# Half of the front projection's chunks by three rounded products, with the key and value rows parked in DRAM, and a reordered end of a down projection

## The reference, cut to what matters

```
h = rmsnorm(x, norm_g)
q, kvc, kvs, kvw, gt, z, xbc, dtr = split_cols(h @ w_in, EVEN_SPLITS)
...
o_nsa = nsa_mixer(q, sigmoid(gt), past_cmp + kvc, past_slc + kvs, win + kvw, ...)
o_ssm, ssm_new, conv_new = mamba_mixer(z, xbc, dtr, conv0, ssm0, ...)
x = x + jnp.concatenate([o_nsa, o_ssm], axis=-1) @ w_out
...
x + (jax.nn.silu(g) * u) @ w_down
```

## Time and profile before

| what | value |
|---|---|
| median of three runs | 2692.76 us |
| profiled execution | 2691.72 us, span 2689.5 us |
| PE busy | 2628.4 us, 98% of the span |
| DVE / ACT / POOL busy | 59% / 42% / 38% |
| x, q, z pieces (L633) | 242.4 us busy, 150.6 to 475.2 us |
| longest wait of PE | 6.6 us, L2358 for DVE L3203, at 1610 us |

### The profile page before, as it was taken

One profiled execution on the slowest core, in us unless ns is written; L12 is line 12 of the kernel. 1 busy time (PEld: TensorE's weight loads), 2 busy tenths in 40 slices (PEclk: granted clock), 3 DMA queues, 4 the chain that ended last, 5 costly groups with the idle time before them and its releaser, 6 DMA issues.

```text
span 2689.5 us, 51117 instructions
## 1 busy us (share of the span) xinstructions
PE 2628.4 (98%) x20404; PEld 2372.7 (88%) x20404; DVE 1589.9 (59%) x2577; ACT 1131.1 (42%) x2373; POOL 1019.5 (38%) x844
## 2 busy tenths in 40 slices
PE   8999999999989999999999999999999999999998
PEld 6866667666669999999999999978999999999998
DVE  3222256777554576667677772186277666676775
ACT  4022213666552644444434342076164444443335
POOL 2431000222223388777730021236148777771000
PEclk9999999999999999999999999999999999999999
DMA  7754310310434222223276331100313222238533
GB/s 234 206 168 155 93 32 1 116 33 2 121 104 155 73 94 93 98 87 116 94 246 205 92 90 41 35 21 17 97 53 113 94 97 98 85 102 295 165 92 105
DMA packets 256591, 283.78 MB, mean 106 GB/s; under 512 B 43098, under 2 KB 192656, under 8 KB 255507
## 3 DMA queue, kind: packets, MB, share of 16 engines
q1 hardware_dynamic: 245840, 247.84, 29.3%
q0 software_dynamic: 7616, 30.14, 3.7%
q10 hardware_dynamic: 2898, 2.54, 0.3%
HBM read 214.25 MB, written 71.32 MB: 106 GB/s over the span
## 4 chain that ended last, share of the span: by engine, by line
PE 65%; DVE 4%; issue 1%; POOL 1%; ACT 1%; DMA 1%; SPq 0%; DVEq 0%; POOLq 0%; ACTq 0%
PE ps L2541 31%; PE ps L3114 16%; PE ps L2342 8%; PE ps L2358 3%; PE ps L3454 1%; PE ps L3314 1%; DVE part L2701 1%; PE ps L3435 1%; PE ps L3418 1%; PE ps L2045 1%; PE ps L2010 1%; PE ps L1998 1%; DVE d_blo L3058 0%; DMA arena<-in_w_gate_up 0%; DVE spot L3229 0%
## 5 line engine op out<-in xcount | busy, mean ns | idle before, releaser
L2541 PE MATMUL ps<-part,block_hi 128*128 128x272 f32 x4768 | 792.1, 288 | 6.8 <-POOL block_lo L2829 5.6
L2541 PEld LDWEIGHTS ps<-part,block_hi 128*128 128x128 f32 x4768 | 675.6, 189 | 8.0 <-issue 7.3
L2541 PE MATMUL ps<-part,block_lo 128*128 128x272 f32 x2672 | 531.0, 289 | 0.0
L2829 POOL TENSOR_TENSOR block_lo<-arena,block_hi 128x512 fp32r<-128x512 f32 x296 | 444.6, 1532 | 51.2 <-ACT block_hi L2596 44.6
L2541 PEld LDWEIGHTS ps<-part,block_lo 128*128 128x128 f32 x2672 | 409.1, 189 | 1.0 <-issue 1.0
L3114 PE MATMUL ps<-d_bhi,d_whi 128*128 128x272 f32 x1232 | 255.1, 288 | 1.3 <-POOL d_wlo L3063 0.8
L3114 PE MATMUL ps<-d_blo,d_whi 128*128 128x272 f32 x1232 | 255.2, 288 | 0.0
L3114 PE MATMUL ps<-d_bhi,d_wlo 128*128 128x272 f32 x1232 | 254.5, 288 | 0.0
L633 PE MATMUL ps<-arena 128*128 128x352 f32 (+1 forms) x768 | 242.4, 473 | 0.0
L2596 ACT CAST block_hi<-arena 128x512 fp32r<-128x512 f32 x296 | 167.1, 619 | 151.7 <-POOL arena L2844 90.8
L633 PEld LDWEIGHTS ps<-arena 128*128 128x128 f32 x768 | 144.4, 191 | 85.0 <-issue 3.8
(11 more groups left out here) (516 smaller groups left out, 4671.1 us busy)
## 6 DMA issues: line engine op xcount, KB each, us to landing
arena<-in_w_gate_up SPq DMA_DIRECT2D x176, 256.0 KB, 3.8
spare_sb<-a_keep SPq DMA_DIRECT2D x78, 272.0 KB, 2.8
arena<-a_keep SPq DMA_DIRECT2D x64, 272.0 KB
arena<-in_w_down SPq DMA_DIRECT2D x16, 1024.0 KB, 7.1
a_keep<-arena SPq DMA_DIRECT2D x58, 272.0 KB, 2.1
arena<-in_cache_nsa_slc_kv SPq DMA_DIRECT2D x112, 128.0 KB, 2.5
a_keep<-spare_sb SPq DMA_DIRECT2D x52, 272.0 KB, 2.0
arena<-in_cache_nsa_cmp_kv SPq DMA_DIRECT2D x109, 128.0 KB, 2.3
```

Source lines behind the costliest of these rows:

```text
L2541: mm = nc.tensor.matmul(ps[:, b + j, 0:QT], y, z[:, j * QT:(j + 1) * QT], start=first and m == 0, stop=last and m == 2)
L2829: p.tensor_tensor(block_of(q, "lo", a), block_f[q % 2]["lo", a], block_of(q, "hi", a).bitcast(F32), ALU.subtract).then_inc(sem("up_lo"), 1)
```

## The change

In every x, q and z piece, the first four chunks (`FK`) are no longer one plain float32 matmul but three rounded ones: weights hi x input hi, weights hi x input lo, weights lo x input hi. The other four chunks stay as they were. The parts come from new instructions:

- ACT rounds the four input chunks to `f_hi` (128x1088 each), and DVE subtracts to get `f_lo` (128x1088 each), once.
- For each of the 8 panels 3 to 10, ACT rounds half of it (`high_part`, 128x1024) and DVE subtracts (`low_part`, 128x1024). The calls stand at fixed places in the two engines' programs. PE waits for the DVE part before the panel's first piece.
- Room: there are two panel slots and not three, so that panel n waits until panel n - 2 is done. `f_hi` lies over `kvt`, so that the key and value rows are parked: ACT writes them to a DRAM tensor `kv_keep` before `f_hi` is made, POOL's stores to the outputs read from there, SP loads the keys for the transposes after the last but one panel is done (`turn_key`, 1 MB), and all rows back to `kvt` after the transposes, ahead of `bias_in`.
- At the end of layer 0's down projection, the four `low` calls no longer stand ahead of the evictions, but one behind each.

```
-SLOTS = 3
+SLOTS = 2
...
+        def high_part(act, n):
+            act.wait_ge(w_ready[n % SLOTS], w_count[n])
+            nc.scalar.copy(fw_hi[n % 2], wp[n % SLOTS][:, 0:FK].rearrange("p c n -> p (c n)")).then_inc(sem("f_hi"), 1)
+        def low_part(dve, n):
+            dve.wait_ge(*reached("f_hi", FK + n - FP0 + 1))
+            raw = wp[n % SLOTS][:, 0:FK].rearrange("p c n -> p (c n)")
+            nc.vector.tensor_tensor(fw_lo[n % SLOTS], raw, fw_hi[n % 2].bitcast(F32), ALU.subtract).then_inc(sem("f_split"), 1)
...
+                        for m, (w, x) in enumerate(((fw_hi[n % 2], f_hi), (fw_hi[n % 2], f_lo), (fw_lo[n % SLOTS], f_hi))):
+                            mm = nc.tensor.matmul(out[:, 0:b - a], w[:, c], x[k][:, a:b], start=k == 0 and m == 0, stop=False)
...
                     self.w = self.E.next_panel()
+                    if kind != "kv":
+                        pe.wait_ge(*reached("f_split", FK + self.E.panel - FP0))
...
+            act.dma_start(kv_kept[:, 0:PT], kvt[:, 0:PT]).then_inc(sem("kv_moved"), 16)
+            act.wait_ge(*reached("kv_moved", 32))
+            step_wait(act, "dve", "h_normed")
+            for k in range(FK):
+                nc.scalar.copy(f_hi[k], hT[:, k]).then_inc(sem("f_hi"), 1)
...
             weights(PROJ0)
+            sp.wait_ge(*panel_done[PROJ0 - 2])
+            sp.dma_start(turn_key, kv_kept[:, 0:PT].rearrange("p i (b n) -> p i b n", b=2)[:, :, :, 0:P])...
             sp.wait_ge(sem("keys_tr"), 1)
+            sp.dma_start(kvt[:, 0:PT], kv_kept[:, 0:PT]).then_inc(sem("kv_moved"), 16)
+            sp.dma_start(kvt[0:TS, PT], kv_kept[0:TS, PT]).then_inc(sem("kv_moved"), 16)
             load(sp, "bias_in")
...
                 if c:
                     state_and_output(c - 1)
+                if c in (1, 4):
+                    low_part(dve, FP0 + 6 + c // 4)
...
                 evict(SSM_PIECES[c])
+                if c in (0, 3):
+                    high_part(act, FP0 + 6 + c // 3)
...
-            for u in range(0 if l else QUADS):
-                low(u)
...
                 evict(len(D_ORDER) - 1, 0)
+                low(0)
                 for k in range(1, QUADS):
                     evict(len(D_ORDER) - 1, k)
                     add_square(3 * QUADS + k - 1)
+                    low(k)
```

More of the change, by code:

```diff
@@ L70 @@
 KH = KC // 2
+FK = KC // 2
+FP0 = 3
 HT = T // 2
@@ L231, in build @@
         o_hi_end = rounded(b0, ["o_hi6", "o_hi7"], [T] * 2)
+        f_hi, f_lo = rounded(kv2, [f"f_hi{k}" for k in range(FK)], [T] * FK), spots[0:FK]
+        fw_hi = rounded(w0 + SLOTS * KC * WCOL, ["fw_hi0", "fw_hi1"], [FK * WCOL] * 2)
+        fw_lo = [rounded(w0 + s * KC * WCOL, [f"fw_lo{s}"], [FK * WCOL])[0] for s in range(SLOTS)]
         PART, BLOCK = KH * HT, KH * P
@@ L415, in dense_slot, with totals @@
             return (n + (n >= DOWN[0])) % WSLOTS
-        def totals(pieces, slots, slot_of):
+        def totals(pieces, slots, slot_of, first=None):
             total, out = [0] * slots, []
             for n, p in enumerate(pieces):
-                total[slot_of(n)] += 16 * len(p(wp[0] if n or slots == WSLOTS else w_kv0))
+                total[slot_of(n)] += 16 * len(p(first if first is not None and n == 0 else wp[0]))
                 out.append(total[slot_of(n)])
             return out
-        w_count, wd_count = totals(panels, SLOTS, lambda n: n % SLOTS), totals(dense, WSLOTS, dense_slot)
+        w_count, wd_count = totals(panels, SLOTS, lambda n: n % SLOTS, w_kv0), totals(dense, WSLOTS, dense_slot)
         wd_ready = [sem(f"wd_ready{k}") for k in range(WSLOTS)]
@@ L632, in one @@
                         a, b = SPLIT[i]
-                        mm = nc.tensor.matmul(out[:, 0:b - a], self.w[:, k, u % 2 * P:(u % 2 + 1) * P], hT[:, k, a:b],
-                                              start=k == 0, stop=k == KC - 1)
+                        if k >= FK:
+                            mm = nc.tensor.matmul(out[:, 0:b - a], self.w[:, k, u % 2 * P:(u % 2 + 1) * P], hT[:, k, a:b],
+                                                  start=False, stop=k == KC - 1)
+                            continue
+                        n = self.E.panel - 1
+                        c = slice(k * WCOL + u % 2 * P, k * WCOL + (u % 2 + 1) * P)
+                        for m, (w, x) in enumerate(((fw_hi[n % 2], f_hi), (fw_hi[n % 2], f_lo), (fw_lo[n % SLOTS], f_hi))):
+                            mm = nc.tensor.matmul(out[:, 0:b - a], w[:, c], x[k][:, a:b], start=k == 0 and m == 0, stop=False)
                 if k1 == KC:
@@ L876, in front_dve @@
             i.then_inc(sem("front_dve"), 1)
+            for k in range(FK):
+                dve.wait_ge(*reached("f_hi", k + 1))
+                v.tensor_tensor(f_lo[k], hT[:, k], f_hi[k].bitcast(F32), ALU.subtract).then_inc(sem("f_split"), 1)
+            for n in (FP0, FP0 + 1):
+                low_part(dve, n)
             dve.wait_ge(sem("w1_used"), W1_CHUNKS)
@@ L891, in front_dve @@
                     values_dve(dve, E, 0)
+                if c in (2, 4, 6):
+                    low_part(dve, FP0 + 1 + c // 2)
             keys_dve(dve, E, 1)
@@ L1163, in front_sp @@
             cache_pages(sp, 0, 22, 42)
-            weights(SLOTS)
+            weights(FP0)
             sp.wait_ge(sem("x_spilled"), 16)
@@ L1167, in front_sp @@
             cache_pages(sp, 0, 64, 72)
[L1168 removed]
+            weights(FP0 + 2)
             sp.wait_ge(sem("w1_used"), W1_CHUNKS)
             cache_pages(sp, 1, 80, 104)
[L1171 removed]
+            weights(FP0 + 3)
             cache_pages(sp, 1, 104, 128)
[L1173 removed]
+            weights(FP0 + 5)
             sp.wait_ge(sem("w1_used"), 2 * W1_CHUNKS)
@@ L1291, in turn_keys @@
             n = tile_n(i)
-            return nc.tensor.transpose(key_bank(br, i), kvt[0:n, i, 256 * br:256 * br + P], ident[0:n, 0:n])
+            keys = turn_key[:, i, br] if i < PT else turn_tail[0:n, br]
+            return nc.tensor.transpose(key_bank(br, i), keys, ident[0:n, 0:n])
         def first_keys_pe(pe, piece):
@@ L1379, in ssm_dve @@
             operands(PT)
+            low_part(dve, FP0 + 5)
             dve.wait_ge(sem("s0t_used"), NB)
```

42 lines of the change are left out of this document (29 added, 13 removed), and 2 rows, old and new, of the table SERVED.

## The result

| | before | after |
|---|---|---|
| median of 22 runs each | 2688.95 us | 2696.19 us |
| lowest to highest | 2685.48 to 2699.89 | 2691.54 to 2707.52 |
| ratio, 95% interval | | 1.0024, 1.0014 to 1.0034 |
| the profiled execution, its span | 2691.72, 2689.5 | 2692.47, 2690.8 |

The account below looks back on a forecast made before the run. PE was taken as the bound, but by only 2 to 3 us. A 22.8 us saving on the pieces, less waits, copies and clock loss, summed to +3.3 us on 2691.72 us, giving 2695.0 us, range 2679 to 2708 us.

Parts of the forecast that it names:

- pieces: x, q and z pieces on PE: three rounded products per chunk replace a plain one in 16 units, -22.8 us.
- the compression's weights: Before the first piece: these weights travel at the same time as the parking, +0.5 us (0 to 2).
- second batch's rows: Before the second batch's hidden steps: PE comes earlier and waits for rows POOL lays, copies meeting DVE's taps, +5.5 us.
- ACT's copies: In the scan: ACT's rounding copies delay the first state copy and a shorter filler piece uncovers ACT's chain, +0.85 us.
- turn 1: Scan turn 1: PE's pieces wait for ACT's copy and DVE's subtraction behind its outputs, +4.9 us.
- turn 4: Scan turn 4: PE's pieces wait for ACT's copy and DVE's subtraction behind its outputs, +5.2 us.
- the attention's start: First attention score: bias tables queue behind 2.1 MB of restored rows, +5.5 us (4.5 to 7.5).
- the down projection's end: PE's wait for the last eviction there: new order of subtractions and evictions gives -0.4 us (-3 to +3).
- the clock: PE's granted clock falls behind four new waits, +4 us (bounds 0 and 11).
- Rival 3: Rounded pieces: weight loads set the pace, 12.7 us more for 576 matmuls, sum +16 us, 2708 us; chance 0.05.
- rival 2: Attention's start: restored rows take 16 us, first score 16 us late, sum +14 us, 2706 us; chance 0.06.
- Rival 1: At the new waits: they are covered and most of the gain stays, 2675 us; chance 0.10.

Follow-up runs that it names:

- panel_later: The changed kernel with panel 4 loaded after the first batch's last product, its parts made in the first round of pieces; 1.0010 of the kernel before.
- before_down: The kernel before, with only its down projection's end changed: four banks read first, one subtraction between second and third; 0.9970 of the kernel before.
- three: The changed kernel with bias tables ahead of restored rows, panel 9 and 10 parts a turn earlier, one piece before the second batch's hidden steps; 0.9933, 2672.8 us.
- down_last: The changed kernel with the down projection's four banks read first, one subtraction between second and third, the rest behind; 0.9990 of the kernel before.
- five: The changed kernel with tables first, parts earlier, one piece moved ahead, panel 4 later and the down projection's banks read first; 0.9903 of the kernel before, 2662.7 us.
- bias_first: The changed kernel with the two bias tables loaded ahead of the restored key and value rows; 1.0008 of the kernel before.
- low_early: The changed kernel with the parts of panels 9 and 10 made a turn ahead of their use; 0.9976 of the kernel before.

## Why the prediction was right, point by point

2695.0 us was forecast and 2696.19 us measured; the working gave +3.3 us and the runs +6.5 us. That the two times lie 1.2 us apart is in part luck: the forecast was added to one execution of 2691.72 us, 2.8 us above the median of the 22 runs before, and its sum was 3.2 us too small. The terms, in us, by the stages above:

| term | forecast | measured |
|---|---|---|
| pieces | -22.8 | -21.9 (16 units of 1.37, read between the hidden steps) |
| the compression's weights | +0.5 | +2.3 (mean of ten traces; 1.2 in the profiled one) |
| second batch's rows | +5.5 | +3.75 |
| ACT's copies | +0.85 | +0.9 (0.46 before the key products, 0.4 in the turns) |
| turn 1 | +4.9 | +4.6 (0.95 and 3.69) |
| turn 4 | +5.2 | +4.7 |
| the attention's start | +5.5 | +6.9 |
| the down projection's end | -0.4 | -0.7 |
| the clock | +4 | +5.7 (1.05 rows, 2.25 turns, 2.36 attention) |
| sum | +3.3 | +6.3 |

- **The pace of the pieces** was right to 4%: rounded matmuls at 0.16 to 0.17 us as in the earlier trace rows. Rival 3, that the weight loads would set the pace, is refuted. The pass rule of the Trainium skill (FP8 and Floating Point Precision, TensorE Precision Notes) gave an estimate of 1.85 us a unit; the trace gives 1.37 us, so the measured pace of another stage was the better source.
- **The weights of the compression** are the term that was mis-sized: +2.3 us, outside the 0 to 2 us that I gave. I had taken the parking as the only load there. With two slots, panel 4 starts at 122.45 us, as the parking does at 123.02 us, and I did not put the two together. panel_later shows that the loss goes when panel 4 is moved. The making of the parts cost nothing, as forecast: PE does not wait before its first piece.
- **The rows**: both halves were right in kind. POOL's copies did meet DVE's taps (6.58 us for 4.68), as the page SBUF — State Buffer of the Trainium skill has it (SBUF: two separate sides). But POOL began them 55.7 us behind the first piece (57.0 us before), and PE's first piece itself stood 2.7 us later than in the kernel before (153.31 against 150.57 us), while the copies began only 1.5 us later; so the wait was 3.75 us and not 5.5. One step here was wrong: I had called SP's wait for the sixth piece free, by 1.4 us, and SP waited 1.8 us, with the second batch's pages behind it. Without that, PE's wait would be up to 1.8 us shorter, an estimate; no run tests it.
- **Turns 1 and 4** came as worked out, to 0.5 us, in place, cause and size.
- **The attention's start** lay within its bounds (4.5 to 7.5). The restored 2048 KB landed in 8.0 us; rival 2, which needed 15.5 us, is refuted.
- **The down projection's end** came as worked out, and I took it for done. What before_down shows is that the same place held 8 us that the change did not touch (L1649 to the first products: 1132.30 us before, 1124.32 us there).
- **Rival 1**, covered waits, is refuted by the four waits themselves. Its 2675 us is what `three` reaches once they are covered.
- **Slips that move no term**: the measured pace is above that of the pass rule by 12 ns a matmul (0.106 us over the 9 matmuls of a chunk), not 15. The windows of the earlier trace rows put the fall of the clock at about 1612.3 us and its return at 1622.5 us, 5.7 us after PE began again.
- What is not settled: which of ACT's small waits belong to the copies, and 0.2 us of the sum. The start-up differs between executions by more than any term but the pieces (the row transposes begin between 120.67 and 131.41 us), so single executions prove nothing about the total.

## What to carry to other kernels

When a full engine is made faster, list whoever stands within a few microseconds behind it at each meeting point; what it gains is lost there until their work moves ahead of it too, and here moving two small instructions by a turn was worth more (11.6 us by the traces, 13 us by the times) than the whole change cost (6.5 us). Queue what is needed first ahead of what is large. And put every transfer of a changed stage on one time line: a store that is free alone (2.1 MB) stood beside a load of 1 MB, and a third transfer came late.

## What the runs showed of the hardware

- After a wait the granted clock went to its lower level (0.50, 1.2 GHz) while or just after PE stood idle, and stayed there for 3.4 to 10.3 us: in the changed kernel from 372.7 to 379.6 us around a wait of 3.69 us, from 215.7 to 219.1 us behind the rows' wait of 3.75 us, and from 481.9 to 492.2 us around a wait of 6.21 us. The waits of 1.12 us at the down projection (down_last, before_down, five) left it at 1.00, but behind one of 1.28 us it was at 0.50 for 3.5 us (bias_first, 483.2 us).
- The clock also fell with PE busy. In low_early (373.1 to 376.5 us) and in the kernel before (397.1 to 400.5 us) it went to 0.50 right at the end of the scan's scores, 32 matmuls of 128x32 in 3.7 us, with no wait of over 0.2 us ahead of them in that turn. In turn 1 of the changed kernel these scores stand ahead of the wait of 3.69 us, so the low stretch there need not be all the wait's.
- A DVE operation with two inputs in SBUF (128x1088, 1.34 us alone) took 5.13 and 5.65 us behind POOL's 128x2048 subtraction, four times its length. Operations that read PSUM beside the same POOL work kept their 0.7 us. It holds the other way too: POOL's copy of 128x2048 took 1.90 us with DVE idle and 2.97 us behind a DVE subtraction that had begun first (changed kernel, 1601.54 and 1608.06 us).
- 2048 KB written to DRAM beside a 1024 KB load took 10.8 us to land, and 6.6 us without it (panel_later, five); read back, 8.0 us ahead of the tables and 10.8 us behind them (bias_first).
